# Two tiles' first feed-forward blocks moved ahead of later layers of the first tiles, in a kernel whose whole order is written out by hand

## The reference, cut to what matters

```
h = h + 0.5 * swiglu(rmsnorm(h, ffn1_norm_g[i]), ffn1_w_in[i], ffn1_w_out[i])
hn = rmsnorm(h, mix_norm_g[i])
if i % 2 == 0:                                   # layer 0: recurrent block
    x_br, g_br, q_mem = split(hn @ lru_w_in[j])  # 768, 768, 256 columns
    xc = causal_depthwise_conv(x_br, ...)        # width 4 along the tokens
    tok = rg_lru(xc, ...) * gelu(g_br)           # linear recurrence along the tokens
else:                                            # layer 1: forgetting attention, causal
    tok = forgetting_attention(q, k, v, f_logit, ...)
cross = memory_cross_attention(q_mem, mem_k, mem_v)   # 256 memory tokens
h = h + concatenate([tok, cross]) @ mix_w_out[i]
h = h + 0.5 * swiglu(rmsnorm(h, ffn2_norm_g[i]), ffn2_w_in[i], ffn2_w_out[i])
```

## Time and profile before

| | us |
|---|---|
| median of 3 runs (lowest, highest) | 5232.4 (5229.44, 5233.56) |
| profiled execution, its time | 5253.84 |
| span of its slowest core (core 5) | 5252.3 |
| spans of the 8 cores | 5202.1 to 5252.3 |
| TensorE (PE) busy | 4961.9 (94%) |
| VectorE (DVE) / ScalarE (ACT) / GpSimd (POOL) busy | 2644.3 / 2585.1 / 964.1 |

### The profile page before, as it was taken

One profiled execution on the slowest core, in us unless ns is written; L12 is line 12 of the kernel. 1 busy time (PEld: TensorE's weight loads), 2 busy tenths in 40 slices (PEclk: granted clock), 3 DMA queues, 4 the chain that ended last, 5 costly groups with the idle time before them and its releaser, 6 DMA issues.

```text
span 5252.3 us, 102855 instructions; the slowest of 8 cores (5202.1 to 5252.3 us)
## 1 busy us (share of the span) xinstructions
PE 4961.9 (94%) x33617; PEld 2717.0 (52%) x33617; DVE 2644.3 (50%) x4498; ACT 2585.1 (49%) x3868; POOL 964.1 (18%) x1219
## 2 busy tenths in 40 slices
PE   7868898899999999999999999999999999999979
PEld 3333353554454655555555554555555555455545
DVE  4355544455455565556544565565444565444324
ACT  2156221547433373535554455664555584556681
POOL 1121211122212220212021111221111221121130
PEclk9989999989999999999999999999999999999999
DMA  8788898888997986688666565666566575566644
GB/s 180 160 204 183 205 234 201 220 195 176 206 250 211 246 231 207 183 236 240 219 198 183 181 221 176 197 177 207 191 187 194 178 218 165 163 211 215 182 135 152
DMA packets 383316, 1039.70 MB, mean 198 GB/s; under 512 B 42736, under 2 KB 62448, under 8 KB 382800
## 3 DMA queue, kind: packets, MB, share of 16 engines
q1 hardware_dynamic: 344640, 904.95, 56.3%
q0 software_dynamic: 38160, 128.17, 16.0%
HBM read 1015.06 MB, written 146.05 MB: 221 GB/s over the span
## 4 chain that ended last, share of the span: by engine, by line
PE 80%; DMA 6%; DVE 5%; ACT 5%; issue 3%; POOL 1%; SPq 0%; DVEq 0%; ACTq 0%; POOLq 0%
PE ps L979 80%; ACT sb_f L988 2%; DMA sb_w<-wf 2%; ACT sb_b L988 2%; DMA sb_w<-wts 2%; DVE sb_f L1022 1%; DVE sb_b L1005 1%; DMA wstr<-sb_w 1%; DVE sb_b L1022 1%; DMA sb_w<-wstr 1%; ACT L988 1%; DVE sb_w L1005 1%; DMA sb_f<-cumrows 0%; DVE sb_f L1005 0%; SPq L235 0%
## 5 line engine op out<-in xcount | busy, mean ns | idle before, releaser
L979 PE MATMUL ps<-sb_b,sb_w 128*128 128x512 bf16 (+1 forms) x23424 | 4349.6, 344 | 138.2 <-DMA sb_w<-wts 45.8
L979 PEld LDWEIGHTS ps<-sb_b,sb_w 128*128 128x128 f16 x23424 | 2265.6, 99 | 2059.4 <-issue 391.2
L988 ACT ACTIVATE sb_f<-ps 128x512 f32<-128x512 f32 x752 | 446.1, 597 | 1122.9 <-PE ps L979 1066.1
L988 ACT ACTIVATE sb_b<-ps 128x1024 bf16<-128x1024 f32 (+2 forms) x908 | 788.0, 930 | 350.3 <-PE ps L979 348.5
L1022 DVE SCALAR_TENSOR_TENSOR sb_f<-sb_f,ps 128x512 f32<-128x512 f32 x704 | 481.2, 683 | 742.0 <-ACT sb_f L988 648.5
L1022 DVE SCALAR_TENSOR_TENSOR sb_f<-ps,sb_f 128x512 f32<-128x512 f32 (+3 forms) x752 | 415.3, 583 | 840.2 <-PE ps L979 821.2
L1005 DVE TENSOR_TENSOR sb_b<-sb_f,ps 128x512 bf16<-128x512 f32 x704 | 483.9, 687 | 328.8 <-PE ps L979 283.9
L988 ACT ACTIVATE sb_f<-sb_f 128x512 f32<-128x512 f32 (+1 forms) x619 | 374.6, 624 | 524.1 <-DVE sb_f L1022 357.1
L1005 POOL TENSOR_TENSOR sb_f<-sb_f 128x512 f32<-128x512 f32 x276 | 361.9, 1313 | 1058.6 <-ACT sb_f L988 1043.7
L1022 DVE SCALAR_TENSOR_TENSOR sb_b<-sb_f,sb_vecs 128x512 bf16<-128x512 f32 (+1 forms) x392 | 291.9, 784 | 87.8 <-ACT sb_f L988 85.3
L1005 POOL TENSOR_TENSOR sb_vst<-sb_vst,sb_enc 128x1040 bf16<-128x1040 bf16 (+1 forms) x96 | 166.7, 1738 | 857.3 <-DMA sb_vst<-vcache 844.4
(11 more groups left out here) (68 smaller groups left out, 1712.1 us busy)
## 6 DMA issues: line engine op xcount, KB each, us to landing
sb_w<-wf SPq DMA_DIRECT2D x685, 512.0 KB, 5.5
sb_w<-wstr SPq DMA_DIRECT2D x784, 352.0 KB, 4.9
sb_w<-wts POOLq DMA_DIRECT2D x199, 512.0 KB, 10.3
wf<-sb_w SPq DMA_DIRECT2D x113, 512.0 KB, 9.4
wstr<-sb_w SPq DMA_DIRECT2D x112, 352.0 KB, 6.2
sb_vst<-vcache SPq DMA_DIRECT2D x96, 260.0 KB, 4.0
sb_f<-cumrows SPq DMA_DIRECT2D x96, 256.0 KB, 6.7
sb_kst<-kcache SPq DMA_DIRECT2D x96, 256.0 KB, 5.8
```

Source lines behind the costliest of these rows:

```text
L979: self.fw.op("pe", lambda e: e.matmul(out_ap, lhsT, rhs, start=start, stop=stop, skip_group_check=True), reads=reads, writes=[ps], signal= ...
L988: self.fw.op("act", lambda e: e.activation(o, i, func, **kw), reads=[in_b] + list(extra), writes=[out_b] + list(also), cost=(func, ns))
```

## The change

Three things change in the program that is built (the costs of some operations and an unused warm-up hook, whose `spin` is 0, change no instruction by themselves).

1. Tiles 2 and 3 get a task `p_t` between `a1_t` and `lru_t`: it parks the residual in `hpark` (8 stores of 256 KB on SP's queue, giving back 8 F pages), and `lru_t` begins by loading it back (8 loads). `x_3` may start once `p_2` is done, `lru_2` once `p_3` is done.
2. `PLAN` is another table. Its start, to the load of tile 4, is another order: `a1_2` runs between `a1_0`/`a1_1` and `lru_0`, `a1_3` between `a2_1` and `b1_0`. After that the order of tasks is nearly that of before. `STORE` is another table as well: counted to the start of `a2_3`, loads of 512 KB from `wts` go from 184 to 157, loads from `wf` from 149 to 178, stores to `wf` from 98 to 96, parks and loads back of 256 KB from 24 and 16 to 40 and 32, result stores from 8 to 11. In the whole program 25 loads go from `wts` to `wf`, and 16 parks and 16 loads back are added; matmuls are the same 33610.
3. The convolution takes its buffer by channel block instead of from the ring.

```
+    "spin": 0.0,
+    "park": (2, 3),
+    "order": {'x_3': ('p_2',), 'lru_2': ('p_3',)},
...
 STORE = (
-    "0000000002000000002000----------------0010000000000000202200----------------0002002002200121120112"
-    "----------------1222201021212112112220----------------2002222200001012020202020"
+    "0000000000100000010100----------------0000000000000000000002----------------0000000000100111111111"
+    "----------------2222122220122211111212----------------0000222201000000000000000"
...
-x_0 +x_1 x_0*6 +mem x_0*5 mem*2 x_0*5 mem*2 x_0 x_1 +a1_0 mem a1_0 mem a1_0*17 mem*4 x_1 mem*2 x_1 mem +x_2 x_1*2
...
@@ tt, stt @@
-                   cost=(None, 155 + (0.521 if fast else 1.042) * n if eng == "dve" else 190 + 2.11 * n))
+                   cost=(None, (165 + 0.6 * n if fast else 155 + 1.042 * n + (0 if a_b.psum or b_b.psum else 70)) if eng == "dve"
+                         else 190 + 2.11 * n))
...
+        ns += 0 if in0_b.psum or in1_b.psum else 55
@@ mix_lru, conv @@
-                xb = self.xbr.next()
+                xb = self.xbr.bufs[c % 3]
@@ _plan @@
         def lru(t):
             def make():
+                if t in self.conf["park"]:
+                    yield ()
+                    self.unpark(t, H[t])
                 n = norm("a2", t)
                 yield from self.mix_lru(t, H[t], N["m0", t], n)
...
+        def rest(t):
+            def make():
+                yield ()
+                self.park(t, H[t])
+            return make
...
-            add(f"x_{t}", first(t))
+            add(f"x_{t}", first(t), self.conf["order"].get(f"x_{t}", ()))
             addf("a1", t, "x")
-            add(f"lru_{t}", lru(t), [f"a1_{t}"])
+            last = f"a1_{t}"
+            if t in self.conf["park"]:
+                add(f"p_{t}", rest(t), [last])
+                last = f"p_{t}"
+            add(f"lru_{t}", lru(t), [last] + list(self.conf["order"].get(f"lru_{t}", ())))
```

More of the change, by code:

```diff
@@ L68 @@
 HOP = 100.0
+SPIN_NS = 216.0
 TABLES = {AF.Tanh: "exp", AF.Ln: "log"}
@@ L156, in pe_free, with _gap @@
         return max(self.q["pe"].quad)
+    def _gap(self, q, reads, writes, cost):
+        toks = [b.lw for b in reads if b.lw]
+        toks += [t for b in reads if b.psum for t in b.rd.values()]
+        for b in writes:
+            toks += ([b.lw] if b.lw else []) + list(b.rd.values())
+        at = max([t[3] + HOP for t in toks if t[2] is not q], default=0.0)
+        before = max(q.quad)
+        return before, at - before
     def op(self, qname, fn, reads=(), writes=(), signal=True, cost=(None, 600.0)):
         q = self.q[qname]
+        if q.is_pe and self.warm:
+            self.warm(*self._gap(q, reads, writes, cost))
         end = self._run(q, self._deps(q, reads, writes), cost)
@@ new lines @@
+a1_0 x_2 a1_1.a a1_0*2 mem a1_0 x_2 a1_1.a a1_0*3 a1_1.a*3 a1_0 a1_1.a a1_1.b a1_1.a*2 x_2*4 a1_1.a*2 a1_0*3 a1_1.b
+x_2 a1_1.b +a1_2 a1_2.a a1_0*7 a1_2.a*2 mem a1_2.a a1_1*8 a1_0 a1_1*2 a1_0*2 a1_2.a a1_1 a1_2.a*2 a1_1*2 a1_2.a a1_0
+a1_1 a1_0 a1_1 a1_0*4 a1_2.a a1_1 a1_0 a1_2.a +lru_0 lru_0 a1_2.a*6 a1_1*2 lru_0 a1_2.a*2 a1_1 a1_2.a a1_1*3 a1_2.a
+a1_1 lru_0 a1_1*13 lru_0 a1_2.a lru_0 a1_2.a*3 +lru_1 lru_1*2 lru_0 lru_1 a1_2.a*3 a1_2.b*2 a1_2.a lru_1*2 a1_2.a*2
+a1_2.b a1_2.a*5 lru_1*4 a1_2.a*2 lru_1.e*2 a1_2.a lru_1.e lru_1.f a1_2.a*2 lru_1.e a1_2.a a1_2.b lru_1.f a1_2.b
@@ new lines @@
+lru_0*4 lru_1.c lru_1.a lru_0*4 lru_1.b lru_1.c lru_1.a lru_0*5 lru_1.d lru_1.b lru_1.d lru_1.b +a2_0 lru_1.c*2
+lru_1.d lru_1.c a2_0*2 lru_1.c a2_0*3 lru_1.c a2_0 lru_1.c a2_0 lru_1.d a2_0 lru_1.c a2_0 lru_1.b*2 a2_0 lru_1.d a2_0
+lru_1.d*2 lru_1.b a2_0*2 lru_1.c a2_0 lru_1.c a2_0 lru_1.d a2_0*5 lru_1.d*2 a2_0 lru_1.d a2_0*2 lru_1.b a2_0 lru_1.d
+a2_0 lru_1.b a2_0*2 lru_1.d lru_1.b a2_0 lru_1.b a2_0*5 lru_1.d a2_0*2 lru_1.d a2_0*3 lru_1.d a2_0*2 lru_1*6 a2_0
+lru_1 a2_0 lru_1*2 a2_0*2 lru_1*2 a2_0 lru_1*4 a2_0 lru_1*2 a2_0 lru_1 a2_0*4 +a2_1 a2_1.a*5 a2_0 a2_1.a*2 a2_0 a2_1.a
@@ L1120, in fill, with warm @@
             self.mm(X, X.ap, self.ones_b, b.hf if half else b.ap, True, True, [self.cb, b])
+    def warm(self, now, gap):
+        if gap < SPIN_NS * 2.0 or not self.PS.free_list:
+            return
+        b = min(self.PS.free_list, key=Buf.idle)
+        at = b.idle()
+        if at > now + 100.0:
+            return
+        fw = self.fw
+        q = fw.q["pe"]
+        fw._deps(q, [self.cb], [b])
+        x = self.cb.ap[:, 0:256].unsqueeze(1).to_broadcast([128, 2, 256])
+        for _ in range(int(gap * self.conf["spin"] / SPIN_NS)):
+            q.prog.append(("op", lambda e, o=b.ap: e.matmul(o, self.ones_b, x, start=True, stop=True, skip_group_check=True),
+                           False))
+        tok = (q.sem, q.count + 1, q, at)
+        b.lw, b.rd = tok, {}
+        self.cb.rd["pe"] = (q.sem, q.count + 1, q, self.cb.rd["pe"][3] if "pe" in self.cb.rd else 0.0)
     def mmk(self, ps, out_ap, w, col, xn, n=TT):
@@ L2156, in _build @@
         self._prologue()
+        if self.conf["spin"] and not self.dry:
+            self.fw.warm = self.warm
         self._plan()
```

590 lines of the change are left out of this document (299 added, 291 removed).

## The result

The changed kernel's four executions take 5168.9, 5169.6, 5199.3 and 5703.0 us, a median of 5184.4; the kernel before, run on the same chip, has a median of 5233.0. The ratio is 0.9895, with a 95% interval of 0.9851 to 0.9939; timed a second time it was 0.9879 (0.9855 to 0.9902). The forecast was 5164 us, a gain of 68; the ratios make it 55 and 63. The profiled execution took 5199.3 us.

The account below looks back on a forecast made before the run. The prediction took DMA waits and the bare recurrent block to bound the kernel, mainly between 213 and 1480 us. Gains of 32 + 1 + 15 + 15 + 5 = 68 us from 5232.4 gave 5164 us, range 5095 to 5240 (forecast's own 5110 to 5215).

Parts of the forecast that it names:

- 213 to 345, +32: 213 to 345 us, 52 lost: `a1_2` beside both output parts covers waits; 32 us gained, 20 remain lost; bounds 0 and 47.
- 345 to 560, +1: 345 to 560 us, 54 lost: the hole moves to a bare `lru_0` rather than closing; gain 1 us, bounds -75 and +25.
- that rival: Around `lru_0`: recurrent blocks also starve `a2_0`, its operations queueing on ACT and DVE; 76 us more lost, 5240 us, chance 0.12.
- 560 to 1000, +15: 560 to 1000 us, 47 lost: `a1_3` beside `a2_1` and `b1_0` stretches float32 reading; gain 15 us, bounds 0 to 40.
- 1000 to 1200, +15: 1000 to 1200 us, 47.7 lost: DMA savings and `lru_2` begun earlier give 15 us, bounds 0 to 40.
- Cost 0; 10 us each for the two tiles if the slots happen to be empty: Parks and loads back of tiles 2 and 3: added waits cost 0, or 10 us each if the slots are empty.
- 1200 to 1480, +5: 1200 to 1480 us, 24.4 lost: loads formerly ahead of 1200 fall here, so only 5 us gained; bounds -15 to +15.
- 1480 to 1984, no term: 1480 to 1984 us, 6.3 lost: the sum of gains has no term for this stage.
- After 1984, 0 (-10 to +15): From tile 4's input to the end, nearly the same order: gain 0, -10 to +15 us for a new table.
- the prediction's own last sign: Tile 4 to the end: the forecast is wrong if this stretch changes by more than 20.
- The DMA sum: Up to the start of `a2_3`: DMA work falls 19 us of 1720, so almost the same.
- DMA alone: First third set by DMA alone: at an unchanged share of 0.867 the gain is 22 us, 5210 us; chance 0.20.

Follow-up runs that it names:

- e3: Changed kernel with all 22 blocks of the first half of layer 0's weights read as float32 by tile 2's first product too; ratio to the kernel before 0.9940.
- e11: Changed kernel with nine output steps of `b1_0` taken behind `lru_2`'s first matmul steps, one after every third step; ratio to the kernel before 0.9901.
- e4: Changed kernel with every weight block stored to its fp16 copy at its first float32 read; ratio to the kernel before 0.9942.
- e6: Changed kernel with the order of the kernel before from the start of `a2_3` on; ratio to the kernel before 0.9951.
- e9: Kernel before with the changed kernel's order from the start of `a2_3` on, nothing parked; no ratio, spans 20 us under the kernel before.

## Why the prediction was right, and where it was not

- *213 to 345, +32.* Measured 27 to 28 in this stage (35 and 34 less the 8 and 6 of the stage ahead). The 20 us that were to remain lost are the 20 of core 5. e3 shows why: the stretch runs at the pace of its transfers, and the gain hangs on `a1_2` taking its blocks from the fp16 copy, as the sum had it.
- *345 to 560, +1.* The hole moved, and the bare `lru_0` came as foretold: 103 us with a clock of 0.83 and 46 lost, for 90, 0.83 and 41. The stage gave 11 to 12, inside its bounds. `a2_0`, DVE and ACT did not starve: from 520 to 650 us PE is 126.64 of 130 busy at 1.00, so that rival is out.
- *560 to 1000, +15.* Measured 29, inside 0 to 40: PE lost 5 us of 310 from 650 to 960.
- *1000 to 1200, +15.* Here a step failed, "Cost 0; 10 us each for the two tiles if the slots happen to be empty" and "`b1_0` is beside it". The stage lost 2 to 7 us instead of gaining 15, outside its bounds of 0 to 40, because of the hole of 34. I had counted the eight loads and their landing. Beside it stands `b1_0`'s first output part, which isn't cover but the cause: its float32 loads and its stores fill the DMA engines (0.96) just when a recurrent block asks for a residual and new weights. Issues from 930 to 1010 us, core 5:

```profile
sb_w<-wts POOLq DMA_DIRECT2D x12, 352.0 KB, 12.6
sb_f<-hpark SPq DMA_DIRECT2D x8, 256.0 KB, 17.1
sb_w<-wf SPq DMA_DIRECT2D x4, 512.0 KB, 20.0
```

The residual took 17.1 us to land and the weights 20.0, for 9.5 and 7.9 in the earlier trace rows. The 10 us of the bound are what e11 shows without the outputs.
- *1200 to 1480, +5.* Measured 5 to 6.
- *1480 to 1984, no term.* The sum left this stage at nothing, and 35 to 36 us were lost in it. "Loads that were ahead of 1200 now fall here" was the right thought at the wrong place: the float32 blocks and 28 stores of `b2_0`'s output part, which before are issued at column times 1054 to 1182, come at 1274 to 1385, behind the point of before's 1480 us. Column times 1203 to 1475 on core 1, before, then the changed kernel:

```profile
1464.00:1746.00 282.00, 281.07 (x1960) 167.15 (x1959) 151.56 (x280) 96.40 (x159) 61.84 (x84) 1.00 0.87 237
```

```profile
1408.00:1725.00 317.00, 293.37 (x1834) 149.17 (x1833) 168.66 (x302) 128.22 (x202) 73.69 (x114) 0.98 0.92 212
```

That is 0.92 x 317 - 0.87 x 282 = 46 us more of DMA work, and 35 us more of time. No run moves this part by itself; in e4 16 more stores there cost 33 us.
- *After 1984, 0 (-10 to +15).* Measured 20 to 25, just outside; e6 and e9 put it down to the order of the last layers. I took "nearly one order" for one order; by the prediction's own last sign, a change of more than 20 behind tile 4, this part was wrong or at the edge of it.
- *Other signs.* PE's lost time from 560 to 1200 is down by a quarter (95 to 74 and 68), not by a third, and tile 4's input is asked for 18 to 26 us earlier on core 1, not 65.
- *The DMA sum.* 19 us less were reckoned to the start of `a2_3`. At its column time, 1687, the engines have worked 1729 us before and 1731 and 1712 in the two profiles after: between 2 more and 17 less. The gain came all the same. The rival "DMA alone" (5210) reckons with one mean share, and e4 shows that such a sum doesn't hold: 55 us taken from the stretch of 951 to 1203 gave 1 us back.

So the total, 57 and 69 us in the two profiles for 68, holds misses that nearly cancel: some 26 more than forecast up to 1000 us and 20 to 25 in the tail, against 17 to 22 less in the stage of the hole and 35 at `b2_0`. The mechanism of the first part was right; that the rest came out near the forecast is luck.
